# Last output tile of each normed stage in two token halves, and the next stage's leading tiles likewise over their first two input tiles

## The reference

```python
def first_block(...):
    ...
    x = x + gate[:, None] * (x_mix @ w_out[i])      # "out1": 2048 -> 1024
    return rmsnorm(x, final_norm_w)

def hybrid_layer(h, ...):
    h = h + 0.5 * rmsnorm_2(swiglu(rmsnorm_2(h, norm_g[0]), ffn1_gu, ffn1_down), norm_g[1])
    z = rmsnorm_2(h, norm_g[2]) @ w_in
    ...                                             # three mixers over z, joined
    h = h + rmsnorm_2(mixed, norm_g[3])             # mixed = joined @ w_out
    h = h + 0.5 * rmsnorm_2(swiglu(rmsnorm_2(h, norm_g[4]), ffn2_gu, ffn2_down), norm_g[5])
    gate = jax.nn.sigmoid(rmsnorm_2(h, norm_g[6]) @ ple_gate)
    h = h + rmsnorm_2((p_i @ ple_proj) * gate, norm_g[7])
    return h
```

## Time and profile before

| | us |
|---|---|
| median of 3 runs | 2724.27 |
| lowest and highest | 2723.16, 2724.53 |
| the profiled execution, its own time | 2720.72 |
| its span in the trace | 2718.9 |
| PE busy | 2605.8 (96% of the span) |
| POOL, DVE, ACT busy | 1293.8, 1121.1, 997.7 |

### The profile page before, as it was taken

The page is one execution under the profiler, slowest core; times in us unless marked ns, Lnnn a source line. Parts: engine busy times, 40 slices in busy tenths (PEclk is TensorE's granted clock), DMA queues, the critical chain, the costliest instruction groups (busy, mean ns, idle before and its releaser), DMA issues.

```text
span 2718.9 us, 33421 instructions
## 1 busy us (share of the span) xinstructions
PE 2605.8 (96%) x12324; PEld 2086.4 (77%) x12324; DVE 1121.1 (41%) x1680; ACT 997.7 (37%) x1482; POOL 1293.8 (48%) x1664
## 2 busy tenths in 40 slices
PE   6999999899999999999999999999999989999997
PEld 3788777677888877677888877888877757888875
DVE  5588665534222047625221046222018645222025
ACT  5323323434233244454333245333234454332234
POOL 1233467555544544345555555455544335555543
PEclk7999999999999999999999999999999989999999
DMA  6212211132333322112332322332322202333322
GB/s 268 70 55 76 75 43 40 39 119 85 99 101 93 94 80 81 47 55 86 93 94 93 109 87 84 101 93 94 101 85 84 63 19 84 99 93 101 94 94 76
DMA packets 63814, 234.23 MB, mean 86 GB/s; under 512 B 7360, under 2 KB 8000, under 8 KB 63168
## 3 DMA queue, kind: packets, MB, share of 16 engines
q1 hardware_dynamic: 61056, 222.33, 26.0%
q10 hardware_dynamic: 2624, 10.00, 1.0%
HBM read 230.00 MB, written 2.10 MB: 85 GB/s over the span
## 4 chain that ended last, share of the span: by engine, by line
PE 84%; DVE 8%; issue 3%; ACT 2%; POOL 1%; DMA 1%; ACTq 0%; SPq 0%; DVEq 0%; POOLq 0%
PE banks L1877 21%; PE banks L1867 21%; PE banks L1868 21%; PE banks L2217 2%; PE banks L2223 2%; PE banks L2218 2%; DVE tmp L1144 2%; DVE sq_sum L1123 1%; DVE xlo L1151 1%; PE banks L1937 1%; PE banks L2338 1%; DVE h L1147 1%; POOL wlo L435 1%; PE banks L2287 1%; PE banks L2289 1%
## 5 line engine op out<-in xcount | busy, mean ns | idle before, releaser
L435 POOL TENSOR_TENSOR wlo<-raw,whi 128x256 fp32r<-128x256 f32 x1584 | 1181.6, 779 | 1273.7 <-ACT whi L538 1273.6
L1867 PE MATMUL banks<-xhi,whi 128*128 128x512 f32 x1920 | 752.6, 392 | 2.3 <-DVE z L1775 2.3
L1868 PE MATMUL banks<-xhi,wlo 128*128 128x512 f32 x1920 | 747.4, 389 | 0.0
L1877 PE MATMUL banks<-xlo,whi 128*128 128x512 f32 x1952 | 735.7, 393 | 10.5 <-DVE xlo L1151 10.4
L538 ACT ACTIVATE whi<-raw 128x1024 fp32r<-128x1024 f32 x396 | 415.2, 1054 | 350.4 <-PE banks L1877 339.9
L1877 PEld LDWEIGHTS banks<-xlo,whi 128*128 128x128 f32 x1952 | 365.2, 188 | 96.7 <-DVE xlo L1151 18.6
L1867 PEld LDWEIGHTS banks<-xhi,whi 128*128 128x128 f32 x1920 | 360.5, 188 | 82.2 <-DVE z L1775 3.2
L1868 PEld LDWEIGHTS banks<-xhi,wlo 128*128 128x128 f32 x1920 | 360.5, 188 | 76.2 <-issue 1.9
L1123 DVE TENSOR_TENSOR sq_sum<-sq_sum,tmp 128x512 f32<-128x512 f32 x110 | 85.3, 775 | 464.6 <-ACT tmp L558 464.6
L1867 PE MATMUL banks<-act_hi,whi 128*128 128x512 f32 x704 | 273.9, 389 | 0.0
L1868 PE MATMUL banks<-act_hi,wlo 128*128 128x512 f32 x704 | 273.9, 389 | 0.0
(11 more groups left out here) (419 smaller groups left out, 3195.5 us busy)
## 6 DMA issues: line engine op xcount, KB each, us to landing
raw<-in_stream SPq DMA_DIRECT2D x396, 512.0 KB, 3.5
ada_raw<-in_stream SPq DMA_DIRECT2D x24, 512.0 KB, 7.3
h<-in_x ACTq DMA_DIRECT2D x2, 2048.0 KB, 12.1
out<-h SPq DMA_DIRECT2D x4, 512.0 KB, 2.6
ctx_raw<-in_ctx ACTq DMA_DIRECT2D x1, 1024.0 KB, 19.6
dft_t<-in_dft_t ACTq DMA_DIRECT2D x1, 1024.0 KB, 4.8
ple_raw<-in_ple ACTq DMA_DIRECT2D x2, 512.0 KB, 3.5
mixpar<-in_mixpar ACTq DMA_DIRECT2D x2, 384.0 KB, 4.2
```

What stands on the lines that cost most here:

```text
L435: piece = pool.tensor_tensor(wlo[:, i, s], raw[:, i, s], whi[:, i, s].bitcast(F32), ALU.subtract)
L1867: pe.matmul(acc[acc_of[t]][:], whi[:, u % SLOTS, i], x_h, start=(k == 0), stop=False, skip_group_check=split)
L1868: pe.matmul(acc[acc_of[t]][:], wlo[:, u % SLOTS, i], x_h, start=False, stop=False, skip_group_check=split)
L1877: mm = pe.matmul(acc[acc_of[t]][:], whi[:, u % SLOTS, i], x_l, start=False, stop=(k == k_tiles - 1), skip_group_check=leading and m < leads)
```

## The change

Four things are written anew:

1. `last_tile` on PE: output tile 7 of out1, down and out2 is computed in two halves of 256 tokens, all input tiles for half 0 and then all for half 1, each half in a PSUM bank of its own (`second`, `earlier_second`). The sum of squares of half 0 is put into half 1 (before input tile 3 of down, 5 of out2, 6 of out1). The last use of a weight unit is now signalled in half 1.
2. `leading` on PE: the 4 leading tiles go over input tiles 0 and 1 for half 0 and then for half 1, all three passes in halves; the sum of squares of half 1 stands between the first eight matmuls and the next four. From input tile 2 on all is as before. After proj, whose tile 7 is not split, both sums stand ahead of the leading tiles, half after half.
3. ACT: `post_half` does for one half the square, Ln and Exp. `norm_in` does half 0, makes `xhi` of input tiles 0 and 1 for it, converts up to two weight units, and then does the same for half 1. Only then come the copy of tile 7 and the squares of h.
4. DVE: `boundary` renews h and makes `xlo` for input tiles 0 and 1 in half 0, then in half 1; the rest as before, with both first squares added after input tile 2.

The start of the ring of banks moves for the first stage of a layer, and the load of `ple_raw` is issued after `norm_in` of its stage.

```diff
+AHEAD = 2
@@ accumulators
+        elif name[0] == "gu" and name[2] == 0:
+            ring = 2
...
+            if (name == "out1" or name[0] in ("down", "out2")) and m == n - 1:
+                second[t] = 1 if name == "out1" else bank[t - 1]
+                earlier_second[t] = last[second[t]]
@@ ACT
+            def post_half(e):
+                key, name, q, source = post[0]
+                s, dst = half(e), inv_rms[:, half(e)]
+                if e == 0:
+                    act.wait_ge(*after("sq_added", (name, q, KT - 3)))
+                act.activation(tmp[1 + (KT - 1) % 2][:, s], source(e), ACT.Square).then_inc(*done(name, (q, KT - 1, e)))
+                act.wait_ge(*after("summed", (key, e)))
+                act.activation(dst, bank[4 + e][:, 0:HALF], ACT.Ln, scale=1.0 / D, bias=eps).then_inc(*done("log", (key, e)))
+                act.wait_ge(*after("log", (key, e)))
+                act.activation(dst, dst, ACT.Exp, scale=-0.5).then_inc(*done("inverse", (key, e)))
             def norm_in(q, gain):
-                high_parts(units_to(q) + SLOTS - 1)
-                for k in range(KT):
+                for e in range(2):
+                    post_half(e)
+                    for k in range(AHEAD):
+                        act.wait_ge(*after("h_new", (q, k, e)))
+                        act.activation(xhi[:, k, half(e)], h[:, k, half(e)], ACT.Copy, scale=gain[:, k:k + 1])\
+                            .then_inc(*done("x_high", (q, k, e)))
+                    if e == 0:
+                        high_parts(units_to(q) + SLOTS - 1)
+                if last_copy:
+                    last_copy.pop()()
+                for k in range(AHEAD):
+                    squares("h_sq", q, k, h[:, k])
+                for k in range(AHEAD, KT):
                     if k == 2:
                         high_parts(units_to(q) + SLOTS)
@@ y_out
-                for m in range(KT):
+                for m in range(KT - 1):
+                    if m == KT - 2:
+                        high_parts(first_block[stage] // UNIT + KT * k // UNIT)
@@ DVE, boundary
+                for e in range(2):
+                    if e and between:
+                        between()
+                    v.wait_ge(*after("inverse", (post, e)))
+                    for k in range(AHEAD):
+                        renewed(k, half(e), (q_pre, k - 1, e) if k else None, [(q_pre, k, e)] + [(q_pre, k)] * e)
+                    for k in range(AHEAD) if q_pre != "last" else []:
+                        lower(k, half(e), (q_pre, k, e))
+                for k in range(AHEAD, KT + 1):
+                    if k < KT:
+                        renewed(k, slice(0, SEQ), (q_pre, k - 1), [(q_pre, k)])
...
@@ PE
+            def last_tile(stage, k_tiles, leads, hi, lo, sum_half, when):
+                m, t = KT - 1, first_tile[stage] + KT - 1
+                for e in range(2):
...
+                    for k in range(k_tiles):
+                        if e and k == when:
+                            sum_half(0)
...
+                        pe.matmul(dst, w_h, hi(k)[:, half(e)], start=(k == 0), stop=False)
+                        pe.matmul(dst, w_l, hi(k)[:, half(e)], start=False, stop=False)
+                        mm = pe.matmul(dst, w_h, lo(k)[:, half(e)], start=False, stop=(k == k_tiles - 1))
+                        keys = [("unit", u)] * (e and i == UNIT - 1) + [(stage, m, e)] * (k == k_tiles - 1)
...
+            def leading(stage, key, sum_half, pre_sum):
+                for e in range(2):
+                    for k in range(AHEAD):
+                        for part in range(2):
+                            if part and e == 0 and k == 0 and sum_half:
+                                sum_half(1)
+                            for m in range(LEADS):
...
+            def post_sum(key, name, q, e):
+                if e == 0:
                     pe.wait_ge(*after("sq_added", (name, q, KT - 2)))
+                pe.matmul(bank[4 + e][:, 0:HALF], ones, sq_sum[:, half(e)], start=True, stop=False)
+                pe.wait_ge(*after(name, (q, KT - 1, e)))
+                pe.matmul(bank[4 + e][:, 0:HALF], ones, tmp[1 + (KT - 1) % 2][:, half(e)], start=False, stop=True)\
+                    .then_inc(*done("summed", (key, e)))
```

334 lines of the change are left out of this document (188 added, 146 removed).

## The result

The changed kernel takes 2738.53 us (median of 5 runs, 2735.93 to 2739.16), the kernel before, run beside it, 2724.27 us (5 runs, 2719.18 to 2725.66). The ratio is 1.0051, with a 95% interval of 1.0039 to 1.0062: slower by half a per cent. The profiled execution took 2735.93 us with a span of 2734.1, against 2720.72 and 2718.9 before: 15.2 us more span.

What follows compares the result with a forecast made beforehand. DVE's sixth `xlo` after a boundary, not PE's first `xhi` wait, was taken to set the pace. Losses 4.5 + 6.8 + 2.1 + 1.7 = 15.1 us on 2720.72 give 2735.8, plus 3.55 for the median: 2739; range 2722 to 2753.

Steps and rivals of the forecast that it cites:

- What sets the pace: At a boundary, DVE's sixth `xlo` decides the time to the pre-sum, not PE's 2.2 us wait for the first `xhi`.
- the two windows of unequal clock: Two boundaries, one at full clock, one at 0.94, take 28.68 and 28.66 us: a slower PE cost nothing.
- `down`: Four boundaries after `down`: sixth `xlo` at T+22.4 for T+23.0, T 1.75 us later; 1.1 us lost each, 4.5 in all.
- T: Moment when PE could take the next instruction after the last product; forecast 1.75 us later at `down`.
- `out2`: Two boundaries after `out2`: T 1.18 us later, input tile 2 later, four DVE operations slowed; 3.4 us lost each, 6.8 in all.
- `proj`: One boundary, `proj` to the next layer: half 1's square comes behind half 0's `xhi`; 2.1 us lost, bounds 0.5 and 4.
- `out1`: One boundary after `out1`: T 1.5 us later, `xhi` of input tile 2 at T+11.1, nothing won; 1.7 us lost.
- A: Rival at the boundaries: PE's wait is what counts, its 17.7 us go; 13 us faster, 2711; chance 0.10.
- B: Rival: near nothing, weights in time at `down`, `out2` at 1.2; 5 us or less, 2724 to 2729; chance 0.17.
- C: Rival: one more POOL split meets DVE at each of six boundaries; 12 us on top, 2751; chance 0.13.
- a factor (1.23/0.68): DVE operations under a POOL split at `out2` grow by this factor, 0.3 us each; the alternative was a 0.55 us fixed wait.
- the other spacing that the prediction names: Tile 7's halves by the skill's N/2.4 + 2.5 ns: 0.2 us per `down`, the sum 3.4 us lower.

Runs made afterwards that it cites:

- experiments 1 to 3: Kernel before with, in turn: two more PE matmuls behind T (2719.34 us), one more DVE operation per boundary (2727.34 us), tile 7's matmuls in halves (2727.53 us).
- experiment 3: Kernel before, with tile 7's matmuls of `down` and `out2` as pairs of 256 columns and nothing moved; 2727.53 us, once.
- Experiment 5: Changed kernel, first weight unit converted before half 0's `xhi`, `out2`'s before half 0's square, both halves squared at once after `proj`; 2730.83 us, ratio 1.0037.
- experiment 1: Kernel before, with two more PE matmuls (0.86 us) between the first `xhi` and the first leading matmul at each boundary; 2719.34 us, once.

## Why the prediction was right, and where its sizes were off

**What sets the pace** after `down`, `out2` and `proj` was read rightly: experiments 1 to 3 show each side of it, and with it the proof drawn from the two windows of unequal clock held.

**`down`, 1.1 us predicted, 1.43 measured.** T is 1.74 us later, predicted 1.75: 0.87 for the halves (experiment 3) and as much for the sum. The first lead starts at T+0.81, predicted T+0.75; the profile gives "issue" as the end of this wait, but POOL's splits of the unit run just up to it. DVE takes up half 1 at T+3.86, predicted T+3.79. The miss is in the next term: two renewals and two `xlo` take 2.90 us, not 2.66. The second renewal starts 0.98 us after the first, not 0.87, and the second `xlo` waits 0.18 us for ACT's `xhi`. From input tile 2 on 15.94 us, as 16.60 less 0.66 has it; the sixth `xlo` ends at T+22.70, predicted T+22.4.

**`out2`, 3.4 predicted, 3.0 measured.** The timeline of the first one (T = 1231.10):

```profile
1232.89 0.36 PE L1955 MATMUL banks<-xhi,whi 128*128 128x256 f32 x1 [1.64 <-ACT xhi L588]
...
1233.64 1.04 ACT L553 ACTIVATE whi<-raw 128x1024 fp32r<-128x1024 f32 x1
...
1234.58 0.37 ACT L576 ACTIVATE tmp<-banks 128x256 f32<-128x256 f32 x1
1234.76 3.02 POOL L450 TENSOR_TENSOR wlo<-raw,whi 128x256 fp32r<-128x256 f32 x4 [10.57 <-ACT whi L553]
1235.00 0.70 PE L2037 MATMUL banks<-tmp,table 128*128 128x256 f32 x2 [0.49 <-ACT tmp L576]
...
1237.22 0.84 DVE L1176 TENSOR_TENSOR h<-h,tmp 128x256 f32<-128x256 f32 x1
...
1240.01 0.75 DVE L1173 SCALAR_TENSOR_TENSOR tmp<-y_dyn,par,inv_rms 128x512 f32<-128x512 f32 x1
```

T is 1.18 us later (predicted 1.18), the two waits are there, for `xhi` and for the square, and the square stands behind a conversion. DVE takes up half 1 at T+5.6 (predicted 5.65) and input tile 2 at T+8.91, predicted 9.3. Off was the number of operations that POOL's split delays: one (0.84 us for 0.42), not four, because POOL, alone on its way at first, is done with its four by 1237.78. The four operations by 0.3 us became one by 0.42, and the same 0.24 us as at `down` came on top. Experiment 5 shows that the place in ACT's queue is a cause: 1.2 us came back at each `out2`.

**`proj`, 2.1 predicted, 2.74 measured.** The rows (T = 1666.80):

```profile
1666.80 0.70 PE L2035 MATMUL banks<-sq_sum,table 128*128 128x256 f32 x2 [1.38 <-DVE sq_sum L1157]
...
1668.92 0.81 DVE L1173 SCALAR_TENSOR_TENSOR tmp<-y_dyn,par,inv_rms 128x256 f32<-128x256 f32 x1 [2.18 <-ACT inv_rms L580]
...
1671.62 0.40 ACT L576 ACTIVATE tmp<-y_dyn 128x256 f32<-128x256 f32 x1
...
1672.07 0.70 PE L2037 MATMUL banks<-tmp,table 128*128 128x256 f32 x2 [3.71 <-ACT tmp L576]
...
1673.76 0.49 DVE L1173 SCALAR_TENSOR_TENSOR tmp<-y_dyn,par,inv_rms 128x256 f32<-128x256 f32 x1 [1.53 <-ACT inv_rms L580]
```

The chain is the one foretold, with each link somewhat longer: DVE's first operation lies under a split (0.81 for 0.48), half 1 is taken up at T+6.96 for T+6.5, input tile 2 at T+9.87 for T+9.2. Experiment 5, with both squares first, gave 1.2 us back.

**`out1`, 1.7 predicted, 1.5 measured, by another way.** T (624.57) is 1.50 us later, as predicted, and PE starts at T+2.90 for T+3.25. But PE was to be held up by the `xhi` of input tile 2 at T+11.1, and it has no wait at all from its first lead on: that `xhi` is there at 635.00, T+10.4, ahead of PE. What takes the time that the earlier start won is PE's own work. From the first lead to the pre-sum it needs 2.63 us more than before: 0.86 for the sum of half 1, 0.16 for the halves, and 1.6 for the clock, at whose lower level the half-width matmuls from 628.93 to 632.3 start 0.213 us apart. The window has 0.94, and that of the kernel before (619 to 649) 1.00:

```profile
621.00:652.00 31.00, 28.26 (x154) 24.70 (x152) 20.14 (x28) 17.89 (x29) 17.22 (x21) 0.94 0.22 68
```

That the term came out right is luck.

**The sum.** The last norm lost 0.2 us of 0. The errors (1.3 us too little at the four `down`, 0.6 at `proj`, 0.8 too much at `out2`) nearly cancel, which is luck in part: 15.1 us predicted, 16.2 by stretches, 15.2 by the spans. The median lies 2.6 us above the profiled execution, for which 3.55 was taken.

**The rivals.** A is refuted (experiment 1). B needed the weights in time and `out2` at 1.2; the 0.65 us of idle time ahead of the leads and the 3.0 us speak against it. C, more splits in DVE's way: DVE's 15.94 us from input tile 2 on are the same after `down`, `out2` and `proj` as before less one `xlo`, so none was added there; only single operations of half width were met.

**A step that holds otherwise than told.** I let a slowed operation cost a factor (1.23/0.68) and named a fixed wait as the alternative. The rows are for neither as it stands, and they are simpler. Here POOL's piece is on its way when the `xlo` starts, and ends at 1003.21; the `xlo` ends at 1003.76:

```profile
1002.02 1.19 POOL L450 TENSOR_TENSOR wlo<-raw,whi 128x256 fp32r<-128x256 f32 x1
1002.54 1.22 DVE L1180 SCALAR_TENSOR_TENSOR xlo<-h,par,xhi 128x512 fp32r<-128x512 f32 x1
```

All 71 slowed operations of the four kinds (L1157, L1173, L1176, L1180) in the changed kernel's trace, and the 65 of their counterparts in that of the kernel before, end 0.54 to 0.56 us after the piece of POOL's that was under way when they started, or 0.28 us after it where they have 256 columns. Twelve more started in the last 0.2 us of a piece and kept their time. So the operation waits for that piece to end, and how much longer it gets depends on when it starts: 0.42 us for the addition to h (0.84 for 0.42 at half width, 1.11 for 0.69 at full width), 0.25 to 0.55 us for the others. It works the other way round too: an operation that starts ahead of a piece is not slowed, and the piece is (0.94 us for 0.73). All 82 pieces of the changed kernel that started during such an operation end 0.58 to 0.66 us after it:

```profile
1236.70 0.48 DVE L1173 SCALAR_TENSOR_TENSOR tmp<-y_dyn,par,inv_rms 128x256 f32<-128x256 f32 x1 [2.45 <-ACT inv_rms L580]
1236.83 0.94 POOL L450 TENSOR_TENSOR wlo<-raw,whi 128x256 fp32r<-128x256 f32 x1
```

The rule of the Trainium skill (SBUF — State Buffer, SBUF: two separate sides), by which the one that comes first has the shared ports for its whole instruction, agrees with both. With four operations by the fixed wait `out2` would have been predicted worse still; it was the count that decided.

**A number that was wrong.** With the other spacing that the prediction names, 0.0025 us for a pair of halves, the sum would be 4.0 us lower (360 matmuls by 0.011 us), not 3.4. The Trainium skill (TensorE: Matmul & The Clock Gate, Back-to-back issue gap) gives that formula for a single matmul by itself, and in these kernels each matmul has a weight load of its own (x12324 of both in the earlier trace rows), so the rows speak of another case. The spacing of 0.120 us held in tile 7.

## What to carry to other kernels

An engine that is busy 96% of the time can wait in a place where it doesn't matter. Before shortening such a wait, look at the next one: if the engine waits again, by the same producer, some microseconds later, and its clock's dips leave the stretch as long as ever, then only work taken from that producer counts. Splitting a chain in two halves has a price even where the number of sums and inverse roots stays the same: narrower matmuls and the first half's sum now stand in a stretch where PE is the bound (1.74 us at each `down`), and the second half's square comes later in ACT's queue, behind the first half's work. Work moved to the engine with slack is good for just that slack: by the medians one sum of squares gained 5 to 6 us and three lost 10, and at the one boundary where PE had no slack even one sum cost 2.5 us.
